# A four-layer sequence model on one core: SSD input products in three 256-column pieces, and the gating's sums over tiles added up on GpSimd

## The chip, the cores and the metric

One core of one Trainium2 chip runs the whole program. The metric is the device time of one execution in microseconds, as the median of the runs. Lower is better.

## The reference, cut to what matters

All is fp32, with 256 positions (S) and a model width of 2048. Four layers follow one another: an LRU and mLSTM layer, an SSD layer, and two layers of attention with spatial gating, each with a gated feed-forward part. The change touches the SSD layer's input product and the gating.

```python
def ssd_layer(x, w_in, conv_w, conv_b, dt_bias, a_log, d_skip, gnorm, w_out):
    u = x @ w_in                                   # 2048 -> 4096 (z) + 6144 (xbc) + 64 (dt)
    z, xbc, dt = jnp.split(u, [D_INNER, D_INNER + SSD_CONV_DIM], axis=-1)
    xbc = jax.nn.silu(causal_conv(xbc, conv_w, conv_b))
    ...
    y = ssd_scan(xh, dt, a, bm, cm) + d_skip * xh  # 64 heads in 8 groups
    y = rmsnorm((y * jax.nn.silu(z)) by group)
    return y @ w_out

def second_block(...):
    for l in range(DEPTH):
        h = rms_norm(x, norm1_g[l])
        q, k, v, gu, gv = jnp.split(h @ w_in[l], splits, axis=-1)
        ...
        sgu = chunked_spatial_gating(jax.nn.gelu(gu), jax.nn.gelu(gv), ln_g[l], ln_b[l], w_s[l], b_s[l])
        mixed = jnp.concatenate([rms_norm(attn, attn_out_g[l]), rms_norm(sgu, sgu_out_g[l])], axis=-1)
        x = x + mixed @ w_o[l]
        x = x + conv_gated_ffn(rms_norm(x, norm2_g[l]), w_up[l], conv_w[l], conv_b[l], w_down[l])

def chunked_spatial_gating(u, v, ln_g, ln_b, w_s, b_s):
    vn = layer_norm(v, ln_g, ln_b)                 # mean and variance over 1024 features
    f = jnp.einsum('hpq,bcqhd->bcphd', w_s, vn) + b_s
    return u * f
```

## The kernel before

Everything lies transposed: features on the 128 partitions, positions on 256 columns (T). A tile of an activation is 128 x 256.

**Products.** `schedule` lists jobs. A job makes one output tile of 128 features from 16 to 32 blocks, and a block is one 128 x 128 piece of weight by one input tile. An fp32 value is split into a high part and a rest, both of type fp32r: the weight into WH and WL, the input into two tiles that lie side by side in 512 columns (H, or Y for the output products). A block multiplies WH with both (512 columns) and WL with the high part (256 columns), L531 and L532. A PSUM bank so gets the main sum in columns 0 to 255 and WH by rest in columns 256 to 511. There are four such banks (psG), and job j waits until job j-4 is evicted.

**Chunks and beats.** Eight blocks of weight, 512 KB, are a chunk. SyncE fetches it into one of six RAW buffers, ScalarE copies it to WH (`split_hi`, one of four buffers), VectorE makes WL (`split_lo`, L1281), three chunks ahead of TensorE. Half a chunk, four blocks, is a beat. Each engine's program is one loop over beats in which the same helpers stand in a fixed order, and each piece of other work is bound to a beat by an offset from the end of its job or from an event in `schedule`. No engine leaves its own order; a wait on one engine holds all that stands behind it there. ScalarE's weight copies stand in the even beats, VectorE's splits in the odd ones.

**Evicting a job.** In the job's end beat ScalarE copies columns 256 to 511 to the output's place (`half`, L773). One beat later VectorE adds columns 0 to 255 to it (`evict`, L1310) and multiplies by the norm's factor `rstd` (L1323). For a residual tile VectorE adds both halves to X.

**SSD input.** Jobs dt, then eight groups of sB, sC, four sx, four sz. Tiles sB, sC and sx go through three places `sds` in turn, sz through four `sdz`. The causal convolution of sC, sB and every other sx is GpSimd's (L1763 to L1768), that of the other sx VectorE's (L1291, L1294). ScalarE makes the tanh of the silu (L1099, L1104, L1109, L1113), the heads' exponentials (L1127, L1128) and the roots of the group norm (L793, L795, each with a table load); VectorE multiplies Et for the heads (L1574) and TensorE takes Et for the head products (L672). The events cb, csb, xk, shead, gsum and gnorm count from the end of the group's last sx.

**Gating.** gv and gu jobs, eight tiles each, get their gelu from GpSimd (a polynomial, L1886 to L1890), ScalarE (tanh, L1206) and VectorE (L1658). The event `sgu` lies seven beats after the last gv job. From there: eight fp32 products of the tiles GV with ones sum over the features (`sums`, L555), ScalarE copies the mean, VectorE and GpSimd subtract it, ScalarE squares the tiles (L1217), eight products with ones sum the squares, ScalarE takes the root, VectorE scales, GpSimd adds the bias (L1913). Then each tile is transposed (L745), copied by ScalarE, and multiplied by w_s (L753); VectorE adds b_s, multiplies by gu (event `sgm`), ScalarE squares, and eight more products with ones give the last norm's sum. `colsum` (L516) is a single product with ones. Each fp32 product of 256 columns has two records in the trace.

**Output of attention and gating.** The first SPLIT = 12 of 16 output tiles are made in two jobs, `ra` over the eight attention tiles, then `res` over the eight gating tiles; the rest in one.

```python
                e.matmul(o, wh, x, start=k == 0, stop=False, skip_group_check=True)
                ins = e.matmul(o[:, 0:T], wl, x[:, 0:T], start=False, stop=last, skip_group_check=True)
```

## Time and profile before

| | |
|---|---|
| median of 3 runs | 3478.89 us (3475.84 to 3481.37) |
| the profiled execution | 3480.91 us, its span 3479.0 us |
| TensorE busy | 3414.5 us (98%), weight loads 2967.4 us |
| VectorE, ScalarE, GpSimd busy | 2733.3, 1896.5, 1726.3 us |
| mean granted TensorE clock | 0.998 |

TensorE's products are pipelined, so their durations overlap: the cost of one is the step from its start to the next one's. A weight load is an instruction of its own and lies beside the products. In the tables a line can be that of a helper: L555 is `sums`, L516 `colsum`, L773 ScalarE's `copy`, L531 and L532 are `blocks`.

### The profile page before, as it was taken

What the parts mean: (1) busy time and instruction counts of PE and PEld (TensorE: products, weight loads), DVE (VectorE), ACT (ScalarE), POOL (GpSimd) and SP (SyncE); (2) the same over time, 40 slices, a digit from 0 to 9 for tenths busy, and PEclk for the clock granted to TensorE, in tenths of its full rate; (3) what the DMA queues carried; (4) which work ended last, traced back from release to release, by engine and by line L of the source; (5) the groups of instructions that cost most, each with busy time, mean ns of one, the idle gap of its engine ahead of it and who ended that gap; (6) DMA issues with size and microseconds to landing.
All of it is one profiled execution on the core that took longest, in us unless ns stands there. A gap on an engine that the chain in (4) does not pass through costs nothing.

```text
span 3479.0 us, 52970 instructions
## 1 busy us (share of the span) xinstructions
PE 3414.5 (98%) x19584; PEld 2967.4 (85%) x19584; DVE 2733.3 (79%) x3931; ACT 1896.5 (55%) x2906; POOL 1726.3 (50%) x1473
## 2 busy tenths in 40 slices
PE   8999999999999999999999999999999999999999
PEld 7888788888888888888888888888888888888888
DVE  8769887679999976787888758877688888658875
ACT  6555785455565554775544434444765544444443
POOL 4325772168888832143566306653143666306640
PEclk9999999999999999999999999999999999999999
DMA  5554555655555556544555665566544555665566
GB/s 188 171 166 158 168 182 182 186 196 173 186 175 170 186 165 187 191 140 134 189 192 189 188 193 189 190 185 194 189 139 141 188 189 192 187 191 192 189 187 182
DMA packets 177041, 624.38 MB, mean 179 GB/s; under 512 B 19784, under 2 KB 25616, under 8 KB 175760
## 3 DMA queue, kind: packets, MB, share of 16 engines
q1 hardware_dynamic: 171216, 606.11, 55.3%
q10 hardware_dynamic: 5568, 14.89, 1.2%
q8 instruction: 156, 2.56, 0.3%
q14 instruction: 101, 0.83, 0.1%
HBM read 618.75 MB, written 2.17 MB: 178 GB/s over the span
## 4 chain that ended last, share of the span: by engine, by line
PE 79%; DVE 10%; issue 4%; ACT 3%; POOL 3%; DMA 0%; ACTq 0%; SPq 0%; POOLq 0%; DVEq 0%
PE psG L531 50%; PE psG L532 25%; DVE WL L1281 3%; ACT WH L773 1%; DVE Et L1574 1%; ACT L793 1%; PE psM L555 1%; DVE sdx L1294 1%; POOL SQ L1763 1%; POOL GV L1913 1%; DVE sds L1323 0%; DVE sdx L1586 0%; DVE sds L1310 0%; PE psM L516 0%; DVE Y L1286 0%
## 5 line engine op out<-in xcount | busy, mean ns | idle before, releaser
L531 PE MATMUL psG<-H,WH 128*128 128x512 f32 x6032 | 2148.9, 400 | 16.1 <-DVE H L1288 12.3
L1281 DVE TENSOR_TENSOR WL<-RAW,WH 128x1024 fp32r<-128x1024 f32 (+1 forms) x1162 | 1524.1, 1312 | 481.9 <-ACT WH L773 479.2
L773 ACT ACTIVATE WH<-RAW 128x1024 fp32r<-128x1024 f32 (+1 forms) x1162 | 1214.2, 1045 | 865.7 <-PE psG L532 841.3
L532 PE MATMUL psG<-H,WL 128*128 128x256 f32 x6032 | 1685.0, 279 | 0.0
L531 PEld LDWEIGHTS psG<-H,WH 128*128 128x128 f32 x6032 | 1133.9, 188 | 279.4 <-issue 17.2
L532 PEld LDWEIGHTS psG<-H,WL 128*128 128x128 f32 x6032 | 1141.0, 189 | 3.1
L531 PE MATMUL psG<-Y,WH 128*128 128x512 f32 x2944 | 1035.7, 397 | 1.0 <-DVE Y L1286 1.0
L532 PE MATMUL psG<-Y,WL 128*128 128x256 f32 x2944 | 823.0, 280 | 0.0
L531 PEld LDWEIGHTS psG<-Y,WH 128*128 128x128 f32 x2944 | 552.7, 188 | 130.4 <-DVE Y L1286 1.3
L532 PEld LDWEIGHTS psG<-Y,WL 128*128 128x128 f32 x2944 | 556.5, 189 | 0.5
L1922 POOL TENSOR_SCALAR fou<-fsu,PAR 128x256 f32<-128x256 f32 x88 | 179.2, 2037 | 550.6 <-DVE fsu L1323 550.6
L1834 POOL TENSOR_TENSOR SQ<-X 128x256 f32<-128x256 f32 x75 | 58.8, 784 | 301.1 <-DVE X L1342 301.1
L1763 POOL TENSOR_SCALAR SQ<-fsu,PAR 128x255 f32<-128x255 f32 x176 | 172.1, 978 | 16.9
L1765 POOL TENSOR_TENSOR fou<-SQ,fou 128x255 f32<-128x255 f32 x176 | 162.3, 922 | 14.7
L1763 POOL TENSOR_SCALAR SQ<-sds,PAR 128x255 f32<-128x255 f32 (+2 forms) x96 | 149.5, 1557 | 9.3
L1930 POOL TENSOR_TENSOR fou<-fou,fog 128x256 f32<-128x256 f32 x88 | 130.6, 1484 | 6.9
L1837 POOL TENSOR_TENSOR SS<-SS,SQ 128x256 f32<-128x256 f32 x75 | 113.4, 1513 | 5.9
L773 ACT ACTIVATE fsu<-psG 128x256 f32<-128x256 f32 x88 | 33.9, 385 | 148.2 <-PE psG L532 148.2
L773 ACT ACTIVATE fsg<-psG 128x256 f32<-128x256 f32 x88 | 33.8, 385 | 144.6 <-PE psG L532 144.5
L1886 POOL TENSOR_TENSOR g_t<-g_s 128x256 f32<-128x256 f32 x32 | 46.1, 1441 | 93.0 <-DVE g_s L1323 93.0
L1310 DVE TENSOR_TENSOR fsg<-psG,fsg 128x256 f32<-128x256 f32 x88 | 37.3, 424 | 69.8 <-ACT fsg L773 69.5
L1831 POOL TENSOR_TENSOR SS<-X 128x256 f32<-128x256 f32 x5 | 5.8, 1160 | 145.1 <-DVE X L1342 145.1
(354 smaller groups left out, 3362.0 us busy)
## 6 DMA issues: line engine op xcount, KB each, us to landing
RAW<-in_w_up SPq DMA_DIRECT2D x352, 512.0 KB, 3.7
RAW<-in_w_o_in SPq DMA_DIRECT2D x162, 512.0 KB, 3.7
RAW<-in_w_e_in SPq DMA_DIRECT2D x128, 512.0 KB, 3.6
RAW<-in_w_down SPq DMA_DIRECT2D x128, 512.0 KB, 3.5
RAW<-in_w_in SPq DMA_DIRECT2D x112, 512.0 KB, 3.6
RAW<-in_w_o SPq DMA_DIRECT2D x72, 512.0 KB, 3.6
RAW<-in_w_e_out SPq DMA_DIRECT2D x64, 512.0 KB, 3.8
RAW<-in_w_o_out SPq DMA_DIRECT2D x64, 512.0 KB, 3.7
```

Of the source, the lines that this page charges most:

```text
L531: e.matmul(o, wh, x, start=k == 0, stop=False, skip_group_check=True)
L532: ins = e.matmul(o[:, 0:T], wl, x[:, 0:T], start=False, stop=last, skip_group_check=True)
L773: copy = lambda o, i, scale=1.0: e.activation(o, i, ACT.Copy, scale=scale)
L1281: tt(WL_[c % NRAW][:, 0:n], RAW_[c % NRAW][:, 0:n], WH_[c % NW][:, 0:n].bitcast(F32), SUB).then_inc(sem("wl"), 1)
L1310: ins = tt(o, out_of(kind, i), o, ADD)
L1763: own.up(ts(m, a, s, None, op0))
L1765: return tt(o, m, c, op1)
L1834: own.up(tt(sq, X[n], X[n], MUL))
L1837: step(tt(ss, ss, sq, ADD), "ssq")
L1886: own.up(tt(t, s, s, MUL))
L1922: own.up(ts(o, s, par(key, "fw", 88 + n), par(key, "fb", n), MUL, ADD))
L1930: step(tt(o, o, f_og[p % 2], MUL), "f_mul")
```

## The change

The jobs of the SSD input (NARROW) are made in three 256-column products a block, all summed in columns 0 to 255: WH by high, WL by high, WH by rest. ScalarE's copy for them goes, and VectorE evicts with a single multiplication out of PSUM, in the job's end beat. It now waits for the free place (`place_free`), as ScalarE did. Their end, from which all SSD events and offsets count, is one beat earlier.

In the gating GpSimd adds the eight tiles GV, each after its gelu, into one tile (`gacc`, which is the first of the two places v2), and one `colsum` gives the mean. It does the same with the squares before the last norm. The sum of the squares of GV stays with eight products. `sgu` is 4 instead of 7 beats after the last gv job, the transposes are 1.5 instead of 1.25 beats apart, and the offsets at the end of `sgm` are two beats larger. SPLIT is 13. The V jobs wait for the last sum, since gacc is a place of theirs. Some semaphores are merged (`rows`, `soft`).

```diff
+NARROW = ("dt", "sB", "sC", "sx", "sz")
+SPLIT = 13
...
-                        self.end[j] = b + (kind not in ("res", "ra"))
+                        self.end[j] = b + (kind not in ("res", "ra") + NARROW)
...
-        s0 = S.end_of("gv", l * 8 + 7) + 7
+        s0 = S.end_of("gv", l * 8 + 7) + 4
...
-            S.event("sgt", l * 8 + i, s0 + 21 + i * 5 // 4)
+            S.event("sgt", l * 8 + i, s0 + 21 + i * 3 // 2)
...
+    gacc = v2[0]
...
-                e.matmul(o, wh, x, start=k == 0, stop=False, skip_group_check=True)
-                ins = e.matmul(o[:, 0:T], wl, x[:, 0:T], start=False, stop=last, skip_group_check=True)
+                if kind in NARROW:
+                    e.matmul(o[:, 0:T], wh, x[:, 0:T], start=k == 0, stop=False)
+                    e.matmul(o[:, 0:T], wl, x[:, 0:T], start=False, stop=False)
+                    ins = e.matmul(o[:, 0:T], wh, x[:, T:2 * T], start=False, stop=last)
+                else:
+                    e.matmul(o, wh, x, start=k == 0, stop=False, skip_group_check=True)
+                    ins = e.matmul(o[:, 0:T], wl, x[:, 0:T], start=False, stop=last, skip_group_check=True)
...
-            for _ in at("dt", b - 8):
+            for _ in at("dt", b - 10):
...
+            for l in at("sgu", b - 4):
+                w.wait_ge(sem("gv_sum"), 8 * l + 8)
+                colsum(("mu", l), gacc)
             for k in range(4):
-                for l in at("sgu", b - 1 - k):
-                    w.wait_ge(sem("gelu"), l * 16 + 8)
-                    for i in (2 * k, 2 * k + 1):
-                        sums(("mu", l), i, GV[i], 8)
...
-            for u in at("sgm", b - 1):
-                w.wait_ge(sem("gu_sq"), u + 1)
-                sums(("suq", u // 8), u % 8, gq[u % 4], 8)
+            for u in at("sgm", b - 3):
+                if u % 8 == 7:
+                    w.wait_ge(sem("gu_sum"), u + 1)
+                    colsum(("suq", u // 8), gacc)
...
-                w.wait_ge(sem("small"), small[("gvq", l)].done if i < 4 else sum_done[(("suq", l), i - 4)])
-                e.activation(gq[u % 4], GU[i], ACT.Square).then_inc(sem("gu_sq"), 1)
-            for u in at("sgm", b - 2):
+                w.wait_ge(*((sem("small"), small[("gvq", l)].done) if i < 4 else (sem("gu_sum"), u - 3)))
+                e.activation(gq[i % 4], GU[i], ACT.Square).then_inc(sem("gu_sq"), 1)
+            for u in at("sgm", b - 4):
...
         def evict(kind, i):
 
             o = place_of(kind, i)
-            w.wait_ge(sem("half"), evn[(kind, i)])
+            if kind in NARROW:
+                w.wait_ge(sem("big"), S.done(kind, i))
+                w.wait_ge(sem("rstd"), LAYER[kind] + 1)
+                tt(o, out_of(kind, i), rstd, MUL).then_inc(sem("ev"), 1)
+                return
+            w.wait_ge(sem("half"), halfn[(kind, i)])
...
+            for i in at("gv", b - 4):
+                l, k = divmod(i, 8)
+                w.wait_ge(sem("gelu"), 16 * l + k + 1)
+                if k == 0:
+
+                    w.wait_ge(sem("small"), small[("suq", l - 1)].done) if l else None
+                    e.tensor_copy(gacc, GV[0]).then_inc(sem("gv_sum"), 1)
+                else:
+                    w.wait_ge(sem("gv_sum"), 8 * l + k)
+                    tt(gacc, gacc, GV[k], ADD).then_inc(sem("gv_sum"), 1)
+            for u in at("sgm", b - 1):
+                l, i = divmod(u, 8)
+                w.wait_ge(sem("gu_sq"), u + 1)
+                if i == 0:
+                    w.wait_ge(sem("small"), small[("mu", l)].done)
+                    e.tensor_copy(gacc, gq[0]).then_inc(sem("gu_sum"), 1)
+                else:
+                    w.wait_ge(sem("gu_sum"), u)
+                    tt(gacc, gacc, gq[i % 4], ADD).then_inc(sem("gu_sum"), 1)
```

## Rows read from the trace of the kernel before

**Rows 1.** The page, the chain that ended last: share of the span by engine
```profile
PE 79%; DVE 10%; issue 4%; ACT 3%; POOL 3%; DMA 0%; ACTq 0%; SPq 0%; POOLq 0%; DVEq 0%
```

**Rows 2.** Timeline of TensorE, SSD input: start us, us, engine line op out<-in xcount
```profile
740.63 0.39 PE L531 MATMUL psG<-H,WH 128*128 128x512 f32 x1
740.86 0.27 PE L532 MATMUL psG<-H,WL 128*128 128x256 f32 x1
740.97 0.40 PE L531 MATMUL psG<-H,WH 128*128 128x512 f32 x1
...
742.71 0.39 PE L531 MATMUL psG<-H,WH 128*128 128x512 f32 x1
```

**Rows 3.** TensorE's waits: us in total, times, longest us
```profile
PE psM L672 <- DVE Et L1574: 17.2, 15, 2.3
PE psM L745 <- POOL GV L1913: 4.7, 2, 2.4
PE psM L753 <- ACT GV L773: 4.5, 2, 3.1
PE psM L555 <- ACT gq L1217: 2.3, 2, 1.1
```

**Rows 4.** Stretches: us, busy of PE, PEld, DVE, ACT, POOL, clock, DMA, GB/s
```profile
714.00:1262.00 548.00, 528.42 (x3077) 447.28 (x3075) 487.52 (x666) 314.59 (x529) 445.85 (x369) 0.99 0.55 178
...
990.90:994.40 3.50, 3.50 (x13) 2.96 (x12) 3.36 (x6) 1.06 (x1) 3.22 (x4) 0.52 0.13 32
...
2646.40:2649.90 3.50, 3.50 (x15) 3.12 (x14) 2.79 (x6) 1.46 (x3) 2.46 (x3) 0.51 0.00 0
```

**Rows 5.** Groups of instructions: xcount | busy us, mean ns | idle before
```profile
L555 PE MATMUL psM<-gq,ONE 128*128 128x256 f32 x64 | 18.7, 394 | 2.3 <-ACT gq L1217 2.3
...
L555 PE MATMUL psM<-GV,ONE 128*128 128x256 f32 x32 | 8.2, 379 | 0.0
...
L1902 POOL TENSOR_TENSOR aacc<-aacc,SQ 128x256 f32<-128x256 f32 x14 | 10.9, 782 | 1.1
```

**Rows 6.** Timeline of TensorE in the gating, two sums between blocks
```profile
1566.44 0.28 PE L532 MATMUL psG<-H,WL 128*128 128x256 f32 x1
1566.56 1.02 PE L555 MATMUL psM<-GV,ONE 128*128 128x256 f32 x4
...
1567.65 0.28 PE L532 MATMUL psG<-H,WL 128*128 128x256 f32 x1
```

**Rows 7.** Timeline of GpSimd, SSD input and gating [idle before <-releaser]
```profile
900.87 1.95 POOL L1768 TENSOR_SCALAR sdb<-sds,PAR 128x256 f32<-128x256 f32 x1 [2.65 <-DVE sds L1323]
...
1596.92 3.19 POOL L1913 TENSOR_SCALAR GV<-GV,PAR 128x256 f32<-128x256 f32 x2 [5.71 <-DVE GV L1672]
...
1602.20 4.05 POOL L1913 TENSOR_SCALAR GV<-GV,PAR 128x256 f32<-128x256 f32 x3
```

**Rows 8.** Timeline of ScalarE in the gating [idle before <-releaser]
```profile
1612.30 0.42 ACT L1206 ACTIVATE g_t<-g_t 128x256 f32<-128x256 f32 x1 [6.71 <-POOL g_t L1890]
```

**Rows 9.** Timeline of TensorE's weight loads, the stretch of rows 2
```profile
740.86 0.19 PEld L531 LDWEIGHTS psG<-H,WH 128*128 128x128 f32 x1
740.97 0.19 PEld L532 LDWEIGHTS psG<-H,WL 128*128 128x128 f32 x1
```

**Rows 10.** The same, four loads in a row in the gating
```profile
1609.22 0.54 PEld L753 LDWEIGHTS psM<-WS,GV 128*128 128x128 f32 x4
```

**Rows 11.** Groups of instructions, evictions of the SSD input
```profile
L773 ACT ACTIVATE sds<-psG 128x256 f32<-128x256 f32 x48 | 18.0, 376 | 24.8 <-PE psG L532 24.5
...
L773 ACT ACTIVATE sdz<-psG 128x256 f32<-128x256 f32 x32 | 12.3, 384 | 35.9 <-PE psG L532 35.8
...
L1310 DVE TENSOR_TENSOR sds<-psG,sds 128x256 f32<-128x256 f32 x48 | 19.8, 412 | 0.6 <-ACT sds L773 0.5
...
L1323 DVE TENSOR_TENSOR sds<-sds,RS 128x256 f32<-128x256 f32 x48 | 28.8, 599 | 1.7
...
L1323 DVE TENSOR_TENSOR sdz<-sdz,RS 128x256 f32<-128x256 f32 x32 | 16.3, 509 | 1.1
```

More of the change, by code:

```diff
@@ L23 @@
 TAIL = 4
-SPLIT = 12
+NARROW = ("dt", "sB", "sC", "sx", "sz")
+SPLIT = 13
 GC = 0.7978845608028654
@@ L436, in build @@
     evac = []
-    evn = {}
+    evn, halfn = {}, {}
     for kind, i, _ in S.jobs:
@@ L444, in build @@
             evn[(kind, i)] = len(evn) + 1
+            if kind not in NARROW:
+                halfn[(kind, i)] = len(halfn) + 1
             evac.append((sem("ev"), evn[(kind, i)]))
@@ L592, in lstm @@
                 use = take("ct")
-                w.wait_ge(sem("gate_rows"), 1)
+                w.wait_ge(sem("rows"), 1)
                 for hf in range(2):
@@ L638, in ssd @@
         def ssd(b):
-            for _ in at("dt", b - 8):
+            for _ in at("dt", b - 10):
                 use = take("dt")
-                w.wait_ge(sem("dt_rows"), 1)
+                w.wait_ge(sem("rows"), 2)
                 q = slice(0, 64)
@@ L826, in halves_of @@
                 if n >= 9:
-                    w.wait_ge(sem("gate_rows"), 1)
+                    w.wait_ge(sem("rows"), 1)
                 if n >= 10:
@@ L961, in gates @@
                 w.wait_ge(own.sem, own.n)
-                e.activation(gz[0:4, :], gz[0:4, :], ACT.Ln, bias=KC[0:4, 3:4]).then_inc(sem("gate_soft"), 1)
+                e.activation(gz[0:4, :], gz[0:4, :], ACT.Ln, bias=KC[0:4, 3:4]).then_inc(sem("soft"), 1)
             for _ in at("gates", b - 8):
-                w.wait_ge(sem("gate_rows"), 1)
+                w.wait_ge(sem("rows"), 1)
                 e.dma_start(scr_m[0], gM[0:4, :]).then_inc(sem("st_m0"), 16)
@@ L1084, in ssd @@
                 w.wait_ge(own.sem, own.n)
-                e.activation(dtv[q], dtv[q], ACT.Ln, bias=KC[0:64, 3:4]).then_inc(sem("dt_soft"), 1)
+                e.activation(dtv[q], dtv[q], ACT.Ln, bias=KC[0:64, 3:4]).then_inc(sem("soft"), 1)
             for _ in at("dt", b - 5):
-                w.wait_ge(sem("dt_rows"), 1)
+                w.wait_ge(sem("rows"), 2)
                 e.dma_start(scr_c, dtz[q]).then_inc(sem("st_cs"), 16)
-            for _ in at("dt", b - 9):
+            for _ in at("dt", b - 11):
                 use = small["dt"]
@@ L1216, in gating @@
                             w.wait_ge(sem("small"), sum_done[(("gvq", l), i - 4)])
+                        elif l:
+                            w.wait_ge(sem("gu_sum"), 8 * l)
                         e.activation(gq[i % 4], GV[i], ACT.Square).then_inc(sem("gv_sq"), 1)
@@ L1234, in gating @@
             for i in range(8):
-                for u in at("sgm", b - 5 - i // 2):
+                for u in at("sgm", b - 7 - i // 2):
                     if u % 8 == 7:
@@ L1323, in evict, with place_free @@
             tt(o, o, rstd, MUL).then_inc(sem("ev"), 1)
+        def place_free(kind, i):
+            if kind == "sB" and i:
+                w.wait_ge(sem("x_conv1"), 2 * i - 1)
+            elif kind == "sC" and i:
+                w.wait_ge(sem("x_conv0"), 2 * i)
+            elif kind == "sx":
+                g, k = divmod(i, 4)
+                if k == 0:
+                    w.wait_ge(sem("x_conv1"), 2 * g) if g else None
+                elif k == 3:
+                    w.wait_ge(sem("x_conv0"), 2 * g + 1)
+                else:
+                    w.wait_ge(sem("bc_conv"), 2 * g + k)
+            elif kind == "sz" and i >= 4:
+                w.wait_ge(sem("s_y"), i - 3)
         def evictions(b):
@@ L1327, in evictions @@
                 for i in at(kind, b - 1):
+                    if kind in NARROW:
+                        place_free(kind, i)
                     evict(kind, i)
@@ L1404, in gates @@
                 w.wait_ge(own.sem, own.n)
-                ts(M, M, -1.0, None, MUL).then_inc(sem("gate_rows"), 1)
+                ts(M, M, -1.0, None, MUL).then_inc(sem("rows"), 1)
         def heads(b):
@@ L1515, in ssd @@
                 w.wait_ge(own.sem, own.n)
-                e.tensor_tensor_scan(z, o, v, 0.0, MUL, ADD).then_inc(sem("dt_rows"), 1)
+                e.tensor_tensor_scan(z, o, v, 0.0, MUL, ADD).then_inc(sem("rows"), 1)
                 w.wait_ge(sem("pb"), 16)
@@ L1685, in gating @@
             for i in range(8):
-                for u in at("sgm", b - 4 - i // 2):
+                for u in at("sgm", b - 6 - i // 2):
                     if u % 8 == 7:
@@ L1691, in gating @@
                         stt(GU[i], GU[i], par(f"pc{l}", "sog", i), gr, MUL, MUL).then_inc(sem("gu_n"), 1)
-                for u in at("sgm", b - 6 - i // 2):
+                for u in at("sgm", b - 8 - i // 2):
                     if u % 8 == 7:
```

30 lines of the change are left out of this document (5 added, 25 removed).

## The prediction

> **What bounds the kernel now.** I read four views, in this order. First the chain that ended last: TensorE holds 79% of it, the next engine 10% [rows 1]. So what TensorE executes counts in full, and what another engine does counts only where TensorE waits for it. Then TensorE's timeline in a quiet stretch of the SSD input: six blocks (a 512-column and a 256-column product each) lie between 740.63 and 742.71, so a block takes 0.347 us; the step from a 256-column product to the next is 740.97 - 740.86 = 0.11 us, and from the 512-column one 0.23 us [rows 2]. Third, TensorE's waits: in all the SSD stage only the head products (L672) wait, for VectorE's Et: 17.2 us in 15 waits. The gating waits 4.7 (L745, for GpSimd), 4.5 (L753, for ScalarE) and 2.3 us (L555, for ScalarE), two waits each, one per layer [rows 3]. Last the stretches: from 714 to 1262 us VectorE is busy 487 of 548 us and GpSimd 446; and four stretches of 3.4 us, the first at 990.9 and the last at 2646.4, run at half of the granted clock, that is 1.2 instead of 2.4 GHz, each after one of these waits [rows 4]. At half clock a stretch of 3.4 us does 1.7 us of work, so the four cost some 7 us. The kernel is thus bound by TensorE's own products, with about 36 us of waits and slow clock inside the two stages that the change touches (17.2 + 11.5 + 7).
>
> **The gating's sums, the surest term.** Before, the sum over eight tiles takes eight fp32 products with ones. Of such a product the timeline has two records: GV x32 is 16 products, gq x64 is 32, of which half are the squares of GV, which stay [rows 5]. The change makes one product out of eight for the mean and for the last norm, in two layers: 4 x 7 = 28 products go. The price of one: between the 256-column products at 1566.44 and 1567.65 stand two sums and one block, 1.21 - 0.347 = 0.86 us, so 0.43 us each [rows 6]. They lie on TensorE, on the path: 28 x 0.43 = **-12.1 us**.
>
> What takes their place are 32 GpSimd operations (28 additions, 4 copies). Additions of this shape took 0.78 us [rows 5]; the copy isn't in the trace, and I bound it by 0.78 and 1.6 us, the latter half of the 3.19 us that two tiles took beside a busy VectorE [rows 7]. All 32 are 25 to 51 us of GpSimd, 6 to 13 in each of four places. For the mean they are spread over the eight GV jobs, and the last is wanted four beats (5.6 us) after its tile is there: hidden. For the last norm one falls in each beat of 1.39 us, in a stretch where GpSimd has nothing else but one polynomial; the product waits at most 1 to 2 us there, and I take nothing since the old eight products began as late. If that cover were gone it would cost two waits of about 2 us. A wait is added on ScalarE too (a square waits for the addition three tiles before instead of for a product); behind it are weight copies made three chunks ahead.
>
> **The gating's waits.** The mean's chain now starts three beats earlier against the products. (a) The 2.3 us of L555: ScalarE's squares stood behind the attention's root and its two table loads; most of them now come before it. They go. (b) The 4.7 us of L745: GpSimd added the bias to two tiles at 1596.92, did a polynomial, and went on at 1602.20 [rows 7]. Now that polynomial belongs to a later beat than the additions and the transposes are spaced 1.5 beats instead of 1.25: the third tile is there some 2 us earlier and wanted 1.4 us later. They go. (c) What is late next: the polynomial now stands behind all eight bias additions, and ScalarE's tanh waits for it in order, with the copies for L753 behind it. Such a wait is in the trace, 6.71 us before 1612.30 [rows 8]. I work it out as 0.6 us a layer if GpSimd's additions take 1.0 us, and 5.2 if they take 1.5 (two of them took 3.19 us, three 4.05 [rows 7]). So of 11.5 us I expect 6.5 to remain: **-5 us**, ends 0 and -11.
>
> **The products of the SSD input.** 81 jobs of 16 blocks, 1296 blocks, go from 512 + 256 columns to three of 256: the same 768 columns, but three weight loads for two. Nothing in the trace is a row of three 256-column products of this type, so I bound it. The step after a 256-column product, which includes the next load, is 0.11 to 0.12 us. Three steps are 0.34 to 0.36 against 0.347: -9 to +17 us over 1296 blocks. Loads do come one after another: each takes 0.19 us in its row but the next starts 0.11 us after it [rows 9], and four in a row around L753 took 0.54 us, (0.54 - 0.19) / 3 = 0.117 apart [rows 10]. So a load in every step fits into a step. I take **0**, the middle of what the steps give, since 0.23 is already twice 0.116.
>
> The rows show a load starting with the product before it, at 740.86 both [rows 2, 9]. The Trainium skill speaks against this change here: "TensorE: Matmul & The Clock Gate", part 3 (The mechanism), says a load overlaps running products only when it goes to another group of rows. By it each added load would stand on the path; the rows here disagree, and what it would do is the third rival below.
>
> **The evictions of the SSD input.** ScalarE's 80 copies out of PSUM go, 18.0 + 12.3 = 30 us, and VectorE's second operation of each, 28.8 + 16.3 = 45 us; the product with rstd now reads PSUM itself, at the 0.41 us that the addition from there took [rows 11] (the 81st, dt, adds one of each). Neither engine bounds, so this is worth only what TensorE's 17.2 us of waits and two slow-clock stretches shrink. VectorE falls from 487 to about 442 of 548 us. GpSimd's chain starts earlier too: at 900.87 it had idled 2.65 us for VectorE's second operation [rows 7], which stood behind ScalarE's copy and a norm, and everything after a job's end is now one beat (1.39 us) earlier. Against it: Et and the exponentials are wanted one beat earlier too, and ScalarE's exponential comes behind a weight copy (1.05 us) in its beat; VectorE's Et in return no longer stands behind a weight split. The wait for a free place moves from ScalarE to VectorE, in front of its splits and Et; ScalarE's copies there waited for TensorE alone (24.5 of 24.8 us, 35.8 of 35.9 [rows 11]), so the place was free in time. I take half of 17.2, without the clock: **-8 us**, ends +3 (the beat works against it) and -20 (all of it and both slow stretches). dt's transposes come two beats later against the earlier end: nothing waits, the first decay is used a group later.
>
> SPLIT 13 puts one more job in two halves per layer: the same 16 blocks, two more VectorE additions of 0.41 us beside free time, 0 us.
>
> **Sum.** -12.1 - 5 + 0 - 8 = -25 us against the profiled execution's 3480.9 (span 3479.0): 3455.8. The median of the runs, 3478.9, is 2.0 below that execution, so I forecast **3454**. A measurement of this kernel can't tell a change within 0.2%, 7 us, from none.
>
> **The rivals.**
> 1. Only the products go: the waits change their place and not their sum, since GpSimd (446 of 548 us) and the order in ScalarE set them. Then 3480.9 - 12.1 - 2 = 3467. For it: none of the GpSimd convolutions is shorter, and the wait in (c) may grow. Against: VectorE is the engine waited for at L672. Chance 0.22.
> 2. GpSimd's new work and the beat moved forward cost back what the products bring: 5 us a layer at L753 (all of the 11.5 us stay), two waits of 2 us at the last norm and +3 in SSD. -12 + 4 + 3 = -5: 3474. Chance 0.07.
> 3. The slower one: the third load paces TensorE. At L531/L532 of the SSD stage the step t of three 256-column products decides: 1296 x (3t - 0.347) outweighs the 25 us gained from t = 0.122 us, and is 7 us slower from t = 0.124. At 0.13 it is 1296 x 0.043 - 25 = +31 us, 3510; with the third load exposed by one spacing of 0.11, 1296 x 0.11 = +143, 3597. For it: TensorE's loads lie 0.117 apart at the best, so nothing is spare, and the 512-column product was where they could catch up. Against it: the steps of 0.11 to 0.12 with a load in each. Chance 0.06.
> 4. The steps are as short as the shortest, 0.113, and the waits go: -12 - 11 - 9 - 20, up to -50, 3430. Chance 0.07.
> That the change doesn't do what it says can hardly be: the second wh product follows wl's, so it needs its own load.
>
> **How the numbers follow.** The forecast has 0.58 (3444 to 3466). The range 3438 to 3473 leaves out most of rivals 3 and 4 and the end of 2. Faster by over 7 us is the forecast, rivals 1 and 4: 0.87; within it rival 2, 0.07; slower rival 3, 0.06.
>
> **What would show it.** L555 with GV gone and gq at x32, L516 with four more products; TensorE's steps in the SSD stage all 0.11 to 0.12; ScalarE's copies of sds and sdz gone; L672's wait under 10 us; L745's and gq's waits gone and L753's between 1 and 10. Wrong would be a step above 0.12, or L672's wait as large as before, or a new wait of the ones products for GpSimd.

## The result, and the profile after

The changed kernel took 3456.3 us (median of 4 runs, 3451.7 to 3457.4), the kernel before 3478.3 us beside it (3475.8 to 3481.4, 4 runs): a ratio of 0.9935, interval 0.9923 to 0.9947. So it is faster by 22 us, against 25 forecast. The profiled execution has a span of 3455.6 us against 3479.0, 23.4 less. The chain that ended last, share of the span by engine:

```profile
PE 89%; DVE 3%; POOL 3%; ACT 3%; issue 2%; DMA 0%; ACTq 0%; SPq 0%; POOLq 0%; DVEq 0%
```

TensorE holds 89% of it for 79%, VectorE 3% for 10% [rows 1]: what has left the path is VectorE's. TensorE's waits after the change (us in total, times, longest):

```profile
PE psM L763 <- ACT GV L784: 7.6, 2, 3.8
PE psM L565 <- ACT gq L1208: 5.3, 2, 2.6
...
PE psM L682 <- DVE Et L1589: 0.9, 1, 0.9
...
PE psM L755 <- POOL GV L1947: 0.4, 1, 0.4
```

Their lines of before are L753, L555, L672 and L745 [rows 3]. The wait for Et has gone from 17.2 to 0.9 us, that for GpSimd's bias from 4.7 to 0.4. But the ones product's wait for the squares has grown from 2.3 to 5.3, and L763's wait for ScalarE's copy from 4.5 to 7.6. In the gating the waits of these three lines were 11.5 us together and are 13.3.

The products of the SSD input, on TensorE's timeline in a quiet stretch, start us and us:

```profile
800.17 0.28 PE L536 MATMUL psG<-H,WH 128*128 128x256 f32 x1
800.29 0.28 PE L537 MATMUL psG<-H,WL 128*128 128x256 f32 x1
800.41 0.28 PE L538 MATMUL psG<-H,WH 128*128 128x256 f32 x1
...
802.33 0.28 PE L536 MATMUL psG<-H,WH 128*128 128x256 f32 x1
```

Six blocks from 800.17 to 802.33 take 2.16 us, 0.360 a block: every step is 0.120 us, where the forecast took 0.116. The groups of the ones products and of the work that replaced them (xcount | busy, mean ns | idle before):

```profile
L565 PE MATMUL psM<-gq,ONE 128*128 128x256 f32 x32 | 9.3, 418 | 5.3 <-ACT gq L1208 5.3
...
L1936 POOL TENSOR_TENSOR v<-v,gq 128x256 f32<-128x256 f32 x14 | 13.2, 942 | 12.6 <-ACT gq L1220 12.6
...
L1927 POOL TENSOR_TENSOR v<-v,GV 128x256 f32<-128x256 f32 x14 | 10.3, 736 | 25.9 <-DVE GV L1673 25.9
...
L1933 POOL COPY v<-gq 128x256 f32<-128x256 f32 x2 | 1.8, 879 | 2.3 <-ACT gq L1220 2.3
...
L1924 POOL COPY v<-GV 128x256 f32<-128x256 f32 x2 | 0.8, 397 | 4.7 <-DVE GV L1673 4.7
...
L1300 DVE TENSOR_TENSOR sds<-psG,RS 128x256 f32<-128x256 f32 x48 | 19.9, 414 | 1.5 <-PE psG L538 1.2
```

L565 has half the records of before, and GV is gone from it [rows 5]. All of GpSimd's new work is 26.1 us, and TensorE waits for none of it. One operation of 0.41 us evicts an SSD tile [rows 11]. Last, the stretches (us, busy of PE, PEld, DVE, ACT, POOL, clock, DMA, GB/s):

```profile
714.00:1262.00 548.00, 547.07 (x4406) 525.01 (x4405) 446.44 (x609) 301.76 (x463) 438.42 (x378) 1.00 0.55 183
...
1567.00:1570.50 3.50, 3.50 (x9) 2.89 (x10) 2.82 (x7) 2.11 (x5) 0.00 (x0) 0.51 0.00 0
1590.80:1594.30 3.50, 3.19 (x11) 2.90 (x12) 3.22 (x7) 3.08 (x6) 1.81 (x2) 0.52 0.00 0
```

VectorE has 446 us there for 487, GpSimd 438 for 446, and TensorE's idle time is down from 19.6 to 0.9 us [rows 4]. The two half-clock stretches of SSD are gone, but a gating layer has two now, one behind each of its long waits. One more, near 369 us, lies outside what the change touches.

**Where the time went, worked out from the starts of TensorE's products.** Each stage (from the first block product that reads H or Y to the next such change) falls into three parts: *steps*, from one block product to the next; *switches*, from a block product to other work, which hold nearly all waits; and *other*, from each other product to what follows. All in us, before and after:

| stage | steps | switches | other | whole |
|---|---|---|---|---|
| SSD input | 456.5, 465.5 | 27.8, 9.0 | 36.1, 35.7 | 520.6, 509.8 |
| SSD output | 182.3, 177.7 | 3.3, 2.0 | 5.1, 4.7 | 190.4, 184.8 |
| layer 3, input and output | 250.0, 251.0 | 15.3, 17.6 | 36.3, 30.2 | 301.4, 298.8 |
| layer 4, the same | 249.5, 251.5 | 15.0, 16.3 | 36.8, 28.7 | 301.1, 296.7 |

(The parts are cut at slightly other instants than the wholes, by up to 0.4 us.) SSD gave 16.4 us, the gating layers 7.0; all other stages are the same within 0.6.

### The profile page after: what moved, and what is told of

It is laid out like the page before. It is cut to its first block, busy times and chain, and to the rows that moved or that the text cites. A ratio compares the mean times of both kernels' runs of the same rounds, so it can differ in the third digit from the quotient of the medians.

```text
span 3455.6 us, 55350 instructions
## 1 busy us (share of the span) xinstructions
PE 3409.5 (99%) x20824; PEld 3023.2 (87%) x20824; DVE 2685.6 (78%) x3854; ACT 1877.0 (54%) x2825; POOL 1739.7 (50%) x1505
## 4 chain that ended last, share of the span: by engine, by line
PE 89%; DVE 3%; POOL 3%; ACT 3%; issue 2%; DMA 0%; ACTq 0%; SPq 0%; POOLq 0%; DVEq 0%
PE psG L541 48%; PE psG L542 24%; PE psG L536 5%; PE psG L538 4%; PE psG L537 4%; ACT WH L784 1%; DVE WL L1272 1%; PE psM L682 1%; POOL GV L1947 1%; ACT L804 1%; POOL SQ L1778 0%; PE psM L521 0%; PE psM L565 0%; POOL g_t L1901 0%; PE psM L556 0%
## 5 line engine op out<-in xcount | busy, mean ns | idle before, releaser
L541 PE MATMUL psG<-H,WH 128*128 128x512 f32 x4736 | 1687.7, 401 | 16.2 <-DVE H L1279 12.7
L541 PEld LDWEIGHTS psG<-H,WH 128*128 128x128 f32 x4736 | 892.0, 188 | 220.4 <-issue 12.7
L536 PE MATMUL psG<-H,WH 128*128 128x256 f32 x1296 | 372.1, 287 | 0.0
L538 PE MATMUL psG<-H,WH 128*128 128x256 f32 x1296 | 366.4, 283 | 0.0
L536 PEld LDWEIGHTS psG<-H,WH 128*128 128x128 f32 x1296 | 248.2, 191 | 5.1 <-issue 4.8
L538 PEld LDWEIGHTS psG<-H,WH 128*128 128x128 f32 x1296 | 248.3, 192 | 0.0
L1778 POOL TENSOR_SCALAR SQ<-sds,PAR 128x255 f32<-128x255 f32 (+2 forms) x96 | 134.4, 1400 | 9.3
```

The lines of the kernel that those rows point to most:

```text
L536: e.matmul(o[:, 0:T], wh, x[:, 0:T], start=k == 0, stop=False)
L538: ins = e.matmul(o[:, 0:T], wh, x[:, T:2 * T], start=False, stop=last)
L1778: own.up(ts(m, a, s, None, op0))
```

## The experiments

The theory after the result: **T**, that the SSD gain comes from the single eviction, which relieves VectorE; that the narrow products cost time and are hidden behind nothing; and that in the gating one long chain (mean, centring, squares, sum, root, scale, bias, transpose, copy) takes as long as before, so a wait that goes comes back further on. The rivals: the beat moved forward made the SSD gain (**R1**); the narrow products' cost is already covered by another engine's pace, so giving it back gains nothing (**R2**); the gating's waits come from single clashes that one moved offset removes (**R3**). The kernel before was run beside each. The expectations below name their theories with letters of their own.

### e1: the wide products again, evicted once

WH by the input's rest is left out of the result here, as it lands in columns that nobody reads; the amount of product work is that of before.

```diff
-                    e.matmul(o[:, 0:T], wh, x[:, 0:T], start=k == 0, stop=False)
-                    e.matmul(o[:, 0:T], wl, x[:, 0:T], start=False, stop=False)
-                    ins = e.matmul(o[:, 0:T], wh, x[:, T:2 * T], start=False, stop=last)
+                    e.matmul(o, wh, x, start=k == 0, stop=False, skip_group_check=True)
+                    ins = e.matmul(o[:, 0:T], wl, x[:, 0:T], start=False, stop=last, skip_group_check=True)
```

> The changed kernel with the SSD input's blocks again as one 512-column and one 256-column product, all else as changed. The eviction still reads columns 0 to 255 alone, so the product of WH with the input's low part is computed and left out of the result. Theory A (the step is longer with a load in each: 3 x 0.120 = 0.360 us a block after, 0.350 before): SSD input blocks at 0.35 us, and 1296 x 0.010 = 12 us less than the changed kernel, about 3444 us, with L682's wait still under 3 us. Theory B (the blocks cost the same and the stage is paced by something else): the same time as the changed kernel within 3 us, with steps near 0.23 and 0.12 and new waits.

Measured: 3457.8 us (3455.7 to 3460.1, 4 runs), ratio to before 0.9938 (0.9923 to 0.9953): no gain over the change. TensorE's waits:

```profile
PE psM L521 <- POOL sq L1798: 7.8, 3, 3.8
PE psM L762 <- ACT GV L783: 7.5, 2, 3.8
PE psM L564 <- ACT gq L1207: 5.1, 2, 2.6
```

The SSD input stage is 512.9 us, for 509.8. By its parts the steps are 458.2 for 465.5, although two stretches of half clock now lie in them (some +3), so the narrow form does cost some 10 us; but the switches are 18.2 for 9.0. TensorE, quicker, now waits for GpSimd's squares of the group (7.8 us). R2 holds, T's second part falls. And the wait for Et is down to 0.2 us in this stage with the wide products too (1.8 in the whole kernel), so it is the single eviction, with the beat moved forward, that takes it away, and not TensorE's slower pace: with wide products it makes the stage 7.7 us shorter than before, and the narrow products in place of the wide ones another 3.1.

### e2: the evictions one beat later

```diff
-                        self.end[j] = b + (kind not in ("res", "ra") + NARROW)
+                        self.end[j] = b + (kind not in ("res", "ra"))
```

> The changed kernel with the SSD jobs' end counted one beat later again, so that the single eviction and all SSD events stand in the beats of before; the narrow products and the missing ScalarE copy stay. Theory A (the lighter VectorE and ScalarE and the slower products took the waits away): L682's waits stay under 4 us and the time is within 4 us of the changed kernel. Theory B (the other order did it: Et ahead of VectorE's weight split, the chain one beat earlier): waits of 8 to 17 us for Et come back, and 8 to 20 us more time, 3464 to 3476.

Measured: 3459.9 us (3458.2 to 3460.1), ratio 0.9943 (0.9928 to 0.9958). The wait for Et stays away at the old beat:

```profile
PE psM L682 <- DVE Et L1589: 1.9, 1, 1.9
```

The SSD input stage is 509.6 us, as in the change; only the output stage is 189.3 instead of 184.8, with a half-clock stretch at 1221 us after that one wait. So the single eviction made the gain of the input stage, and R1 falls there. The output stage is another matter: its switches and "other" are those of before again (3.3 and 5.1 us, for 2.0 and 4.7 in the change), and of the 5.6 us that it had gained 4.5 are gone. In this one trace most of its gain hangs on the earlier beat. The kernel's 3459.9 us, above every run of the change, fits that.

### e3: the gating's change alone

```diff
-NARROW = ("dt", "sB", "sC", "sx", "sz")
+NARROW = ()
...
+            for x in at("sx", b):
...
+                half("sx", x)
```

(ScalarE's copies of all five kinds are back, with the waits that they had.)

> The gating part of the change alone: NARROW is empty and ScalarE's copies for the SSD jobs are back, so the SSD stage is that of before. By the stages of the two traces the gating brought 7 us: 12 from the 28 products, less 2 of longer waits and 3.4 of two more slow-clock stretches. Theory A (the two parts add): 3471 us, 7 less than before, the SSD stage as before with 17 us of waits for Et. Theory B (the SSD part's gain hangs on the gating or the other way): under 3465 or over 3476.

Measured over 8 runs: 3470.5 us (3469.2 to 3471.7), ratio 0.9975 (0.9965 to 0.9986), so 7 to 8 us of the 22. Its SSD stages take 519.6 and 190.4 us, as before, and the waits are back with them:

```profile
PE psM L682 <- DVE Et L1612: 17.4, 17, 2.3
PE psM L763 <- ACT GV L784: 7.5, 2, 3.8
PE psM L565 <- ACT gq L1231: 5.4, 2, 2.8
```

The two parts of the change are independent: the stages of the gating measure what they do in the change, and those of SSD what they did before.

### e4: the third product at 128 columns

WH by the rest is left out for half of the positions.

```diff
-                    ins = e.matmul(o[:, 0:T], wh, x[:, T:2 * T], start=False, stop=last)
+                    ins = e.matmul(o[:, 0:P], wh, x[:, T:T + P], start=False, stop=last)
```

> A measurement: the third product of each SSD input block takes 128 columns of the input's low part instead of 256, so half of that correction is left out. Theory A (the weight load paces the step): the step after the 128-column product stays at 0.11 to 0.12 us and the time within 8 us of the changed kernel. Theory B (the columns pace it): that step falls to 0.06 us, some 1296 x 0.06 = 78 us less, unless VectorE then bounds the stage.

Measured in one run: 3462.3 us. Timelines of TensorE's products and of its weight loads:

```profile
800.36 0.33 PE L536 MATMUL psG<-H,WH 128*128 128x256 f32 x1
800.53 0.28 PE L537 MATMUL psG<-H,WL 128*128 128x256 f32 x1
800.65 0.22 PE L538 MATMUL psG<-H,WH 128*128 128x128 f32 x1
800.71 0.33 PE L536 MATMUL psG<-H,WH 128*128 128x256 f32 x1
```
```profile
800.30 0.19 PEld L536 LDWEIGHTS psG<-H,WH 128*128 128x128 f32 x1
800.41 0.19 PEld L537 LDWEIGHTS psG<-H,WL 128*128 128x128 f32 x1
800.53 0.19 PEld L538 LDWEIGHTS psG<-H,WH 128*128 128x128 f32 x1
800.65 0.19 PEld L536 LDWEIGHTS psG<-H,WH 128*128 128x128 f32 x1
```

A block with 640 columns takes 0.35 us (0.349 in the mean, outside the stretches of half clock), not 5/6 of 0.360: the short product's step is 0.06 us, but the step after the next product, whose load had started only 0.06 us before it, is 0.17. The loads come 0.349 / 3 = 0.116 us apart in the mean. So neither theory came as written: the short step did fall to 0.06 us, and the block got only 0.01 us shorter. Three loads with their products take 0.35 us even where the columns would ask for less, and three products of 256 columns, at 0.360, lie 0.01 above that. Rival 3 of the forecast named the right part; its step of 0.120 stayed just below the break-even of 0.122. Why it is 0.120 and not the 0.116 of the loads is open. As in e1, what TensorE gains goes to the group's squares (11.6 us in 3 waits, each with 6.8 us of half clock beginning before its end), and the stage is longer, 515.3 us.

### e8: WH with high and rest in a row, WL last

```diff
-                    e.matmul(o[:, 0:T], wl, x[:, 0:T], start=False, stop=False)
-                    ins = e.matmul(o[:, 0:T], wh, x[:, T:2 * T], start=False, stop=last)
+                    e.matmul(o[:, 0:T], wh, x[:, T:2 * T], start=False, stop=False)
+                    ins = e.matmul(o[:, 0:T], wl, x[:, 0:T], start=False, stop=last)
```

> The changed kernel with the three products of an SSD block in the order WH by high, WH by rest, WL by high: the same three loads, two of them of the same weights one after the other. Theory A (each load costs its 0.117 us whatever it brings, so the pace stays): steps of 0.117 to 0.120 us and the same time. Theory B (the chip or the compiler saves a load of weights that are already there): fewer loads in the trace or a step under 0.115.

Measured in one run: 3450.4 us. The SSD input stage is 509.8 us and the median step 0.120, both as in the change: the same weight twice in a row is loaded twice, and nothing is saved. What this execution is shorter by lies where its code is the changed kernel's: 3.1 us in the first output stage (180.1 for 183.2), 4.4 in the two gating layers, which had one half-clock stretch each instead of two. So single times of 3450 to 3457 don't rank such kernels; the stages do, and they too only to some 5 us for the gating: its two layers take 591.1 to 596.5 us in the seven traces with the change's gating (e1 to e4, e8 and e9 with it).

### e5, e6, e7: one offset of the gating moved at a time, then both

The attention's root one beat later (e5); GpSimd's bias additions spread over twice the beats (e6); both (e7).

```diff
-        S.event("attn", l, S.end_of("Q", l * 8 + 7) + 32)
+        S.event("attn", l, S.end_of("Q", l * 8 + 7) + 33)
```
```diff
-                for l in at("sgu", b - 18 - k):
+                for l in at("sgu", b - 18 - 2 * k):
```

> The changed kernel with the attention's event one beat later (Q7 + 33 instead of + 32), so that ScalarE's last two squares of GV come before the attention's root and its two table loads. Theory A (the root, 3.4 us, in front of the last squares makes TensorE wait): the gq wait of 5.3 us falls under 1, the slow-clock stretch behind it goes in both layers (3.4 us), together 7 to 8 us less in the two gating input stages; L763's 7.6 us stay. Theory B (GpSimd's centring and polynomial, for which ScalarE idled 4.75 us before, are what is late): the wait stays above 3 us.

> The changed kernel with GpSimd's bias additions two beats apart instead of one, so that the polynomial of gu 5 stands between the fourth and the fifth of them. Theory A (ScalarE's tanh waits for the polynomial behind all eight additions, and the copy of a transposed tile behind the tanh makes TensorE wait at L763): L763's wait falls from 7.6 to under 2 us and the slow-clock stretch behind it goes, 8 to 10 us less over both layers; the gq wait stays at 5.3. Theory B (the additions themselves are late): the wait moves to L755 with 3 us or more.

> The two edits of e5_attn1 and e6_spread together in the changed kernel. Theory A (two independent waits): about 16 us less than the changed kernel, 3440 us, and the gating's products then bring the 12 us that were forecast for them. Theory B (one wait hides the other, the second grows when the first goes): less than 10 us, over 3446.

Measured: e5 3450.7 us and e6 3459.8 us in one run each, e7 3454.4 us (3450.6 to 3457.9, 4 runs), ratio 0.9938 (0.9921 to 0.9954). The two gating layers take 591.1, 597.2 and 591.5 us, where the change has 595.5 and e8, with the change's own gating, 591.1. The waits of e5, then of e6:

```profile
PE psM L755 <- POOL GV L1947: 5.9, 2, 2.9
PE psM L763 <- ACT GV L784: 5.6, 3, 3.0
```
```profile
PE psM L763 <- DVE GV L1694: 6.7, 2, 3.4
PE psM L565 <- ACT gq L1208: 5.1, 2, 2.6
PE psM L763 <- ACT GV L784: 3.1, 2, 1.5
```

e5 takes away the wait for the squares, and one for the bias appears in its place; e6 takes more than half of the wait for ScalarE's copy, and one for VectorE's addition of b_s appears. In e7 L755 has 5.9, L763 4.3 and 2.7: 12.9 us in all, against 13.3. Each of the two offsets moves its wait and saves none: R3 falls for them. The layers' 591 us in e5 and e7 lie inside the spread of the unchanged gating. That e5 takes L565's wait away shows what made it: the attention's root ahead of the last squares. Where these waits come from stands in the changed kernel's ScalarE timeline, start us, us, [idle before <-releaser]:

```profile
1553.64 0.73 ACT L1208 ACTIVATE gq<-GV 128x256 f32<-128x256 f32 x2 [0.64 <-POOL GV L1941]
...
1555.41 0.70 ACT L1208 ACTIVATE gq<-GV 128x256 f32<-128x256 f32 x2
1560.87 0.42 ACT L1195 ACTIVATE g_t<-g_t 128x256 f32<-128x256 f32 x1 [4.75 <-POOL g_t L1905]
1561.19 0.71 ACT L1208 ACTIVATE gq<-GV 128x256 f32<-128x256 f32 x2
...
1563.13 1.28 ACT L804 ACT_TABLE_LOAD   x1
...
1564.92 1.28 ACT L806 ACT_TABLE_LOAD   x1
...
1566.54 0.71 ACT L1208 ACTIVATE gq<-GV 128x256 f32<-128x256 f32 x2
```

Four squares, then 4.75 us of waiting for a polynomial of GpSimd that itself stood behind the centring, two more squares, and the attention's root with its two table loads ahead of the last pair, for which L565 waits until 1566.99. And further on, GpSimd and ScalarE:

```profile
1577.11 10.43 POOL L1947 TENSOR_SCALAR GV<-GV,PAR 128x256 f32<-128x256 f32 x8 [1.38 <-DVE GV L1687]
1587.51 1.47 POOL L1901 TENSOR_TENSOR g_t<-g_s 128x256 f32<-128x256 f32 x1
1589.07 0.41 POOL L1903 TENSOR_SCALAR g_t<-g_t 128x256 f32<-128x256 f32 x1
1589.56 0.72 POOL L1905 TENSOR_TENSOR g_t<-g_t,g_s 128x256 f32<-128x256 f32 x1
```
```profile
1590.37 0.42 ACT L1195 ACTIVATE g_t<-g_t 128x256 f32<-128x256 f32 x1 [5.20 <-POOL g_t L1905]
1590.70 0.37 ACT L784 ACTIVATE GV<-psM 128x256 f32<-128x256 f32 x1
```

The eight bias additions in a row hold the polynomial until 1587.51, the tanh waits for it, the copy of GV stands behind the tanh, and TensorE's L763 waits 3.8 us for the copy.

### e9: e1 with the group norm three beats later

This asks whether GpSimd's squares alone held e1. The same part is left out as in e1, and one line more is changed:

```diff
-        S.event("gnorm", g, x3 + (57 if g < 7 else 35))
+        S.event("gnorm", g, x3 + (60 if g < 7 else 35))
```

> e1_wide_once with the group norm's event three beats later (x3 + 60 instead of + 57 for groups 0 to 6), so that the product with ones asks 4 us later for GpSimd's sum of squares. As in e1_wide_once the product of WH with the input's low part is left out of the result. Theory A (GpSimd's squares are only late by up to 3.9 us and have slack after it): L521's 7.8 us for GpSimd and the two slow-clock stretches of the stage go, the SSD input stage falls from 512.9 to 500 to 504 us, and the time to about 3446 us: the wide product's 12 us become visible. Theory B (GpSimd's work of a group, 55 of 62 us busy, paces the stage): other waits for GpSimd or Et take their place and the stage stays above 508 us.

Measured: 3453.0 us (3449.0 to 3453.4, 4 runs), ratio 0.9924 (0.9908 to 0.9941). The wait for the squares is gone, and another is there; under it VectorE's timeline before one of these waits, which ends at 903.14:

```profile
PE psM L681 <- DVE Et L1588: 8.6, 7, 1.3
```
```profile
900.44 0.75 DVE L1276 TENSOR_TENSOR Y<-sdx,Y 128x256 fp32r<-128x256 f32 x2
...
902.36 0.63 DVE L1588 TENSOR_TENSOR Et<-Et,CBt 128x384 f32<-128x384 f32 x1
```

The SSD input stage is 508.5 us, 1.3 under the change: the steps give 9.7 (455.8 for 465.5), the switches take back 8.3 (17.3 for 9.0). But this doesn't show that VectorE's Et would have held e1 as well. The wait comes once a group, 1.29 us each time, and the late Et stands behind the group norm's own work on VectorE (L1276), which this edit puts three beats later, without a pause since 894.97; in e1 the same stage waits 0.2 us for Et. So the edit that took one wait away may have made the other. What is shown is that the wide products shorten the stage by no more than 1.3 us in either order, e1's or e9's; whether another order would gain is open.

### e10 and e12: the whole chain given three more beats

Since moving one offset moved only the wait, the consumers were moved: the transposes and what follows them start three beats later, the attention's root one.

```diff
-        S.event("attn", l, S.end_of("Q", l * 8 + 7) + 32)
+        S.event("attn", l, S.end_of("Q", l * 8 + 7) + 33)
...
-            S.event("sgt", l * 8 + i, s0 + 21 + i * 3 // 2)
-            S.event("sgm", l * 8 + i, max(S.end_of("gu", l * 8 + i) + 7, s0 + 30 + i))
+            S.event("sgt", l * 8 + i, s0 + 24 + i * 3 // 2)
+            S.event("sgm", l * 8 + i, max(S.end_of("gu", l * 8 + i) + 7, s0 + 33 + i))
```

> The changed kernel with the attention's event one beat later (as e5_attn1) and the gating's transposes and multiplications (sgt and sgm) three beats later, 4.2 us; the output product wants its gating tiles not before some six beats after them. Theory A (the gating is a chain of fixed length, from the mean to the bias, and TensorE only comes too early for it; it has other blocks to do): the waits at L565, L755 and L763, 13.3 us in the changed kernel and 11.5 in e5_attn1, fall under 4, the two or four slow-clock stretches go, and the four stages of the two layers sum to 576 to 584 us (595.5 in the changed kernel): 3438 to 3444 us. Theory B (the order inside ScalarE and GpSimd, not the beats, is what is late): the waits stay above 8 us or move to the product's input tiles.

Measured: 3458.0 us, but over 10 runs that lie between 3449.2 and 3478.6, ratio 0.995 (0.9929 to 0.9971); the profiled execution took 3476.2. Its waits in the gating:

```profile
PE psM L755 <- ACT GV L784: 3.1, 2, 1.5
...
PE psM L763 <- ACT GV L784: 1.1, 1, 1.1
```

4.2 us are left of 13.3 at these lines, and one half-clock stretch per layer (the first of 6.8 us). But the waits of the blocks for VectorE's weight split have grown, from 3.4 us in 2 waits in the changed kernel:

```profile
PE psG L541 <- DVE WL L1272: 9.8, 6, 3.3
```

Two of them, of 2.83 us, end at 1581.84 and 2622.33, one in each gating layer, where the changed kernel has none. So the gating's waits are 9.8 us and not 4.2, and part of them has moved once more, out of the chain and into the blocks. T's chain of fixed length is not borne out by this: its last part, that a wait comes back elsewhere, is. The two layers take 589.0 us, 6.5 under the change but only 2.1 under the shortest of the seven traces with its gating, where 576 to 584 were expected. What on VectorE makes the split late was not taken apart. And the 20 us above the change's time lie in the feed-forward stages, whose code is the same: 249.3 or 248.7 us for 244.6 or 244.1, and 124.4 for 122.0. The same kernel was run once more for a second trace.

> The kernel of e10 a second time, for one more trace. In e10's profiled execution (3476.2 us) the pairs of a 512-column and a 256-column product of the feed-forward stages began 0.353 us apart at the median stretch, in every other trace of this study 0.347 us, with the same instructions and the granted clock at full speed; its ten times lie between 3449 and 3479. Theory A, the pace of those pairs is a state that an execution falls into and that makes the whole spread: a time near 3447 to 3452 comes with pairs of 0.347 us from 1700 us on and feed-forward input stages of about 244.5 us; a time near 3475 with 0.353 us and 249 us; a time between the two with some stages of each. The input and output stages of layers 3 and 4 then have waits of TensorE of 4 to 5 us together, where the changed kernel had 13.3. Theory B, the spread has another cause (transfers, a stretch of half clock, waits): the time is off 3476 without the feed-forward pairs having changed their pace.

Measured: 3452.3 us, with feed-forward stages of 244.6 and 122.0. The same stretch in e12, then in e10 (columns as above; the first count is TensorE's products):

```profile
2070.00:2290.00 220.00, 220.00 (x1272) 193.97 (x1271) 186.60 (x258) 107.17 (x160) 144.03 (x120) 1.00 0.57 190
```
```profile
2070.00:2290.00 220.00, 220.00 (x1247) 190.72 (x1247) 180.81 (x252) 104.84 (x157) 144.54 (x118) 1.00 0.57 187
```

TensorE has no idle time in either, the clock is at full speed in both, and e10 gets through 2% fewer products. The pairs begin 0.3467 us apart in e12 (230 + 116.7 ns) and 0.353 in e10 (236 + 117). That fits theory A of the expectation: the pace differs from one execution of the same kernel to the next, and it makes the 28 us by which the eight feed-forward stages of e10's profile are longer. With them taken off, it would be 3448, at the low end of its ten times. e12's time lies 0.3 us above the band named. What sets the pace is open, and that it makes the spread of the other times rests on these two traces. The gating layers of e12 are 589.8 us; its waits there are 5.0 us at L763 and 6.4 for the weight split.

### e11: e10, with sz wide and evicted by both engines

```diff
-NARROW = ("dt", "sB", "sC", "sx", "sz")
+NARROW = ("dt", "sB", "sC", "sx")
...
-        S.event("gnorm", g, x3 + (57 if g < 7 else 35))
+        S.event("gnorm", g, x3 + (60 if g < 7 else 35))
...
+            for n in at("sz", b):
+                if n >= 4:
+                    w.wait_ge(sem("s_y"), n - 3)
+                half("sz", n)
```

> e10_later and, in the SSD stage, the sz jobs with wide products and ScalarE's copies again (512 of 1296 blocks) and the group norm three beats later. The narrow blocks cost 0.010 us each more than wide ones, so 5 us less if the lighter VectorE still keeps up: about 5 us below e10_later, the SSD input stage 505 instead of 510 us. The rival (the 32 copies and second operations bring the waits for Et back): the stage stays at 510 us or more.

Measured: 3455.4 us (3454.5 to 3468.2, 4 runs), ratio 0.9944 (0.9922 to 0.9965).

```profile
PE psM L682 <- DVE Et L1593: 8.7, 8, 1.3
```

The SSD input stage is 513.5 us, 3.7 over the change. Four of ten jobs a group are wide again, and the steps are 4.1 us shorter (461.4 for 465.5); but 8.7 us of waiting for Et are back. That need not be the work of the 32 second operations on VectorE: e9 has the same wait of 1.3 us a group without any, and the two share the group norm's later event. The norm's edit and sz's were not tried apart, so e11 doesn't show what the exchange is worth on these tiles. The gating's waits are 10.7 us here, 5.7 of them for the weight split. A version clearly ahead of the changed kernel was not found: e9 leaves out part of the computation, and e10's median is not below the change's.

## Why the prediction was right, and where it was not

The time came within 2.3 us of the forecast, and that is luck: by the stages SSD gave 16.4 us where 8 were forecast, and the gating 7.0 where 17 were, and the two misses cancel. That there is a gain, and that it comes from the lighter evictions and from the products with ones, was right.

- **The gating's products, -12.1.** Right and slightly small: "other" fell by 6.1 + 8.1 = 14.2 us over the two layers. GpSimd's additions took 0.74 and 0.94 us, its copies 0.40 and 0.88, together 26.1 us, the low end of 25 to 51, and no wait for them appeared: the cover named for them was there.
- **The gating's waits, -5.** Wrong in sign: they went from 11.5 to 13.3 us, and two more stretches of half clock (of 3.4 us, some 1.6 lost in each) came with them, so +5 or so. The step that failed is (a), "They go". "Most of them now come before it" was true, six of the eight squares, but the tanh in ScalarE's order held four of the eight for 4.75 us, and the last pair stood behind the root's table loads after all: 2.3 us became 5.3, and with the root one beat later (e5) they are gone. (b), the bias wait, went as forecast, 4.7 to 0.4. (c) was right in kind and size: the polynomial stands behind all eight additions, of 10.43 / 8 = 1.30 us each, and 3.8 us a layer lie inside the 0.6 to 5.2 that were worked out. What was missed over all three is that they are no separate terms: e5 to e7 move a wait along the chain and leave some 13 us or more, and with more time for its later part (e10 to e12) 10 to 11 us remain, half of them at the weight split. Together the gating gave 7.0 us (e3 confirms it by itself: 7 to 8), not 17.
- **The SSD's products, 0.** Mis-sized: 0.120 us a step, the upper end of "0.11 to 0.12". The stage's pairs took 0.351 us in the mean, so the narrow block at 0.360 costs 1296 x 0.009 = 12 us. The row of before was from a quick stretch (0.347), and a step with a load in it came out at 0.120 and not 0.116, though the loads by themselves can come 0.116 apart (e4); what makes the difference is open. On the time itself it cost nothing: put in place of the wide products under the single eviction, the narrow ones make the stage 3.1 us shorter (e1), so the forecast's 0 stands nearer to what an experiment gives than its sum of steps deserved. The rows show loads of 0.19 us that start 0.12 apart and beside a running product, here too. The Trainium skill's rule in "TensorE: Matmul & The Clock Gate", part 3, that a load overlaps only when it goes to another group of rows, would by the loads' spacing here put 0.12 or so on the path in every block, an estimate of 150 us; the trace doesn't bear it out. The same section also names a load into the background weight buffer as one that may run ahead; no run here shows which of the two these loads are.
- **The SSD's evictions and waits, -8.** Right in cause, half in size. The switches fell by 18.8 us and both half-clock stretches went (-3.4): more than the end at -20. But they aren't the eviction's alone: with wide products (e1) they fall by 9.6, and the rest goes with TensorE's longer steps, for which nothing is late any more. I took "half of 17.2" for want of a reason; e1, e2 and e3 show that the single eviction takes the whole wait for Et away, whether by VectorE's 45 us or ScalarE's 30; these two were not taken apart, only that L672 waits for VectorE speaks for the first. With the step's +12 the input stage came out at -10.8. The output stage gave 5.6 more, which the forecast had no term for beside these waits: 1.3 in switches, and 4.6 in steps, the mean pair being 9 ns shorter in it over its 512 blocks. Part of that is the two paces that e10 and e12 show: away from the waits its pairs are 0.353 us apart in the two traces with the old evictions (before and e3) and 0.347 in the twelve with the single one. So it may belong to the change; why is open.
- **The beat moved forward and SPLIT 13** have no part in the input stage, which is as long in e2 as in the change; in the output stage the beat has most of the 5.6 us (e2, one trace). SPLIT was not tried alone.
- **The rivals.** Rival 1 (3467) had the gating right and SSD wrong. Rival 3 had the load's pace right, but 0.120 stayed under its own threshold of 0.122, and e1 shows that even the steps' 10 us weren't lost: taken back, they went to waits for GpSimd and to half clock, and 3 more with them.

## What to carry to other kernels

When one engine is 98% busy and waits a few microseconds for several others, remove operations from the engine it waits for most, and look at what the next one asks for before pricing anything on the first: here 10 us of longer products cost almost nothing, since in e1 and e9 the quicker products mostly waited. Waits along one chain of engines are not separate terms: here each that was moved away came back at another line. So count a saving by the waits of all lines in the stage and by the stage's own time, not by the line whose wait was aimed at, which in e10 would have shown 4.2 us for 9.8. Price a new form of product by the mean over the whole stage, with its loads, not by the shortest stretch.

## What the runs showed of the hardware that was not expected

- Loads of 128 x 128 weights (fp32r, 0.19 us each) come 0.116 us apart in the mean of e4's stage at full clock, where one product in three has only 128 columns; with 256 columns each the steps settle at 0.120. The same weights twice in a row are loaded twice (e8).
- Pairs of a 512- and a 256-column product have two paces at full granted clock with no wait, 0.3467 and 0.353 us. An execution can hold the slower one over all feed-forward stages (e10, +28 us) or in one stage (the first output stage, the same code in all, was 180.1 to 180.3 us in eight traces and 183.2 to 183.3 in six). The spread of e10's times, 29 us, is as large as that.
- With most of TensorE's waits of over 2 us in the gating, and with the waits for the squares in e1 and e4, the granted clock went to half for 3.4 us (6.8 three times in e4), beginning in the wait or within 1.5 us of its end; of the twelve waits of 2.0 to 2.3 us for Et in before and e3 only three had it. Pairs began 0.640 us apart there for 0.347 (e2, from 1221.1 us), so a stretch of 3.4 us costs some 1.6; a wait removed can give it back too, and a wait of 3.8 us is so one of 5.4.
